# Order of the query blocks in the forgetting-attention branch: 0 to 7 against 0, 7, 1, 6, 2, 5, 3, 4

## The reference, cut to what matters

```python
c = jnp.cumsum(log_f, axis=1).transpose(0, 2, 1)
def block(i):                                   # i = 0..7, 128 queries each
    logits = einsum('bqhd,bkhd->bhqk', qb, k) * scale
    logits = logits + (cb[..., :, None] - c[..., None, :])
    logits = where(kpos[None, :] <= qpos[:, None], logits, -inf)
    p = softmax(logits, axis=-1)
    return einsum('bhqk,bkhd->bqhd', p, v)
```

## Time and profile before

| what | us |
|---|---|
| median of 3 runs | 1442.84 |
| the 3 runs | 1442.63, 1442.84, 1447.26 |
| the profiled execution | 1447.09 |
| its span, first to last instruction | 1445.2 |
| PE busy in the span | 1410.0 (98%) |
| DVE busy, ACT busy | 718.6 (50%), 689.4 (48%) |
| branch A, its first logits to its last pv | 660.5 to 893.3 |

### The profile page before, as it was taken

One profiled execution on the slowest core, in us unless ns is written; L12 is line 12 of the kernel. 1 busy time (PEld: TensorE's weight loads), 2 busy tenths in 40 slices (PEclk: granted clock), 3 DMA queues, 4 the chain that ended last, 5 costly groups with the idle time before them and its releaser, 6 DMA issues.

```text
span 1445.2 us, 21066 instructions
## 1 busy us (share of the span) xinstructions
PE 1410.0 (98%) x7910; PEld 1120.0 (77%) x7910; DVE 718.6 (50%) x1628; ACT 689.4 (48%) x1518; POOL 69.0 (5%) x136
## 2 busy tenths in 40 slices
PE   7999999999999999999999999999999999999998
PEld 7977677777767888887778777777777778888786
DVE  7558655555556785464433434633333355222633
ACT  7457866666763351114655565554454523113312
POOL 3132000000000000000000000000000000000100
PEclk9999999999999999999999999999999999999999
DMA  6155111111111222222010121112232131232522
GB/s 212 30 139 155 35 37 38 30 30 38 37 37 30 52 59 74 65 73 74 23 30 23 30 81 52 45 37 74 73 93 83 52 103 44 69 85 66 175 81 102
DMA packets 108019, 96.26 MB, mean 67 GB/s; under 512 B 8464, under 2 KB 93840, under 8 KB 107664
## 3 DMA queue, kind: packets, MB, share of 16 engines
q1 hardware_dynamic: 96672, 58.22, 14.9%
q0 software_dynamic: 11248, 36.71, 8.3%
HBM read 72.62 MB, written 18.09 MB: 63 GB/s over the span
## 4 chain that ended last, share of the span: by engine, by line
PE 84%; ACT 2%; DVE 2%; issue 1%; DMA 0%; DVEq 0%; ACTq 0%; POOL 0%; POOLq 0%
PE bank L855 20%; PE bank L857 20%; PE bank L856 20%; PE bank L1031 7%; PE bank L1050 6%; PE slot L1021 4%; PE slot L1006 2%; PE slot L855 1%; PE slot L856 1%; PE slot L857 1%; PE bank L975 1%; PE bank L1089 0%; DVE hs L1488 0%; ACT hs L1403 0%; PE bank L983 0%
## 5 line engine op out<-in xcount | busy, mean ns | idle before, releaser
L855 PE MATMUL bank<-hs,w_hl 128*128 128x512 f32 x1088 | 436.5, 401 | 0.4 <-issue 0.3
L857 PE MATMUL bank<-hs,w_hl 128*128 128x512 f32 x1088 | 426.6, 392 | 0.0
L856 PE MATMUL bank<-hs,w_hl 128*128 128x512 f32 x1088 | 425.5, 391 | 0.0
L1442 DVE TENSOR_TENSOR w_hl<-w_raw,w_hl 128x512 fp32r<-128x512 f32 (+1 forms) x168 | 113.8, 678 | 285.4 <-ACT w_hl L1141 284.4
L857 PEld LDWEIGHTS bank<-hs,w_hl 128*128 128x128 f32 x1088 | 205.0, 188 | 44.6
L855 PEld LDWEIGHTS bank<-hs,w_hl 128*128 128x128 f32 x1088 | 205.6, 189 | 41.3 <-issue 1.5
L856 PEld LDWEIGHTS bank<-hs,w_hl 128*128 128x128 f32 x1088 | 205.8, 189 | 39.8
L1141 ACT ACTIVATE w_hl<-w_raw 128x512 fp32r<-128x512 f32 (+1 forms) x168 | 103.9, 620 | 160.0 <-PE bank L857 152.1
L1469 DVE TENSOR_SCALAR_CACHE_REDUCE idle_out<-score,state 128x768 uint8<-128x768 f32 (+3 forms) x140 | 115.3, 824 | 4.8
L1649 DVE CUSTOM_DVE_ANT_0 slot<-slot,score 128x128 f32<-128x128 f32 (+7 forms) x64 | 47.4, 780 | 71.1 <-PE slot L1021 71.0
L1340 ACT ACTIVATE idle_out<-score,state 128x896 bf16<-128x896 f32 x64 | 70.3, 1098 | 11.6 <-DVE state L1465 10.3
(11 more groups left out here) (312 smaller groups left out, 2200.0 us busy)
## 6 DMA issues: line engine op xcount, KB each, us to landing
w_raw<-in_w_in_dram SPq DMA_DIRECT2D x136, 256.0 KB, 2.8
merged_scratch<-ms POOLq DMA_DIRECT2D x16, 512.0 KB, 3.5
ms<-merged_scratch POOLq DMA_DIRECT2D x16, 512.0 KB, 4.0
xn<-in_x_dram SPq DMA_DIRECT2D x8, 512.0 KB, 6.1
iq_st<-iq_hl POOLq DMA_DIRECT2D x32, 128.0 KB, 3.0
qb<-qb_scratch POOLq DMA_DIRECT2D x8, 512.0 KB, 5.2
w_raw<-in_w_o_dram SPq DMA_DIRECT2D x16, 256.0 KB, 3.8
qb_scratch<-bq_high POOLq DMA_DIRECT2D x4, 512.0 KB, 3.0
```

What stands on the lines that cost most here:

```text
L855: pe.matmul(out_, wh, mh, start=start, stop=False)
L856: pe.matmul(out_, wh, ml, start=False, stop=False)
L857: return pe.matmul(out_, wl, mh, start=False, stop=stop)
L1442: v.tensor_tensor(lo, src, hi.bitcast(F32), ALU.subtract).then_inc(w_low, 1)
```

## The change

The units of each head pair of branch A are listed in the order of query blocks 0, 7, 1, 6, 2, 5, 3, 4. Three places follow it: the filler of the last pair goes by the position in the pair and not by the block's number; the broadcasts for the first pair stand at steps 0, 0, 1, 1, because block 7 in step 1 reads all keys' gates; and DVE waits for the second half of the broadcasts at block 7. Branches B and C keep their order.

```diff
             elif x["br"] == "a" and x["ch"] == NCH["a"] - 1:
-                pump(1 if x["b"] >= 3 else 0)
+                pump(1 if s % TB >= 3 else 0)
...
-                    before.setdefault(at - 5 + i if ch else (0, 0, 2, 3)[i], []).append(bcast)
-            for b in range(TB):
+                    before.setdefault(at - 5 + i if ch else (0, 0, 1, 1)[i], []).append(bcast)
+            order = (0, 7, 1, 6, 2, 5, 3, 4) if br == "a" else range(TB)
+            for b in order:
...
-                        if a["br"] == "a" and a["b"] in (0, 4):
+                        if a["br"] == "a" and a["b"] in (0, 7):
```

## The result

The changed kernel is slower, by about 0.5%. Its median is 1451.57 us over 6 runs (1449.11 to 1456.11), that of before in the same comparison 1443.70 over 6 runs; the ratio is 1.0051, 95% interval 1.0036 to 1.0065. Two further sets gave 1449.45 (ratio 1.0036, 1.0022 to 1.0050) and 1451.17 (1.0041, 1.0026 to 1.0055). Over all 16 runs the median is 1450.76, that of 23 runs of before 1444.1.

What follows compares the result with a forecast made beforehand. PE, busy 98% of the span, was taken as the bound. New waits of +3.9 us in the last pair and 0.5 in the first, added to the median 1442.84, gave 1447.2 us, range 1442.0 to 1451.0.

Steps and rivals of the forecast that it cites:

- Last pair, item 1: Last pair's start: logits of block 7 wait 0.55 us for block 0's exps, starting 2.45 us after block 0's logits.
- Item 2: Last pair: turn of block 7 needs both its exps, at 8.55 us; PE waits 2.7 us, partly before block 0's pv.
- Item 3: Last pair: logits of block 6 need block 1's exps, queued behind ACT's copies; start at 12.95 us, a 1.9 us wait.
- Sum for the last pair: Last pair's waits 5.5 us, less 1.8 of before that go, plus 0.2 counted on both sides: +3.9 us.
- First pair, 0.5 us: First head pair: two broadcasts behind the value transposes share two banks; two PE waits, together 0.5 us, bounds 0 and 1.1.
- Head pairs 0 to 2, "no new wait": In pairs 0 to 2 filler in every step covers the latencies of blocks 7 and 6, so no new wait.
- The sum, +4.4 us: Branch A: last pair +3.9 and first pair 0.5; waits of steps 24 to 27 bounded by 4.0 and 6.3 us.
- The median of before as the base: The +4.4 us was added to the runs' median 1442.84, not to the profiled execution's 1447.09.
- The clock falls too: Rival: last pair's thinly used PE drops to half clock for about 7 us, giving 1449.6 us; chance 0.25 (1448 to 1451).
- My 2.4 for one fall: Price in us of one clock fall in the last pair: at most 3.4 lost, 2.4 taken since some time is waits anyway.
- the even mix: Rival: narrow units beside each wide one keep ACT and DVE from lagging, waits vanish, up to 2.6 us faster; chance 0.13.
- The waits were not half as long: Rival on the last pair: its chain starts earlier, waits only half as long, +1 to +2.5 us (1443.8 to 1445.3); chance 0.19.

Runs made afterwards that it cites:

- the last pair's order alone: New order only in branch A's last head pair, other pairs ascending as before: 1450.33 us, ratio 1.0035; with 13 unread matmuls added inside its two long waits, 1445.72 us, 1.0013.
- the fill: Unread extra matmuls inside PE's waits; here 13 in the last head pair's two long waits, added to the changed kernel: 1451.73 and 1449.20 us, ratio 1.0039 each.
- the pair of kernels with all waits filled: Changed kernel plus 13 unread matmuls in the last pair and 10 between branches C and A: 1448.84 us; kernel before plus those 10 only: 1444.14 us.

## Why the prediction was wrong, point by point

- *Last pair, item 1.* Right. Logits of block 7 were put 2.45 us behind those of block 0; they start at 846.32-843.90 = 2.42.
- *Item 2.* Right. The turn of block 7 was put at 8.55 and stands at 852.44-843.90 = 8.54. The waits before it are 0.47 and 1.94 us; the list gives 0.3 less than the 2.7 I gave, since the tails of the matmuls hide that much.
- *Item 3.* Right. The logits of block 6 were put at 12.95 and stand at 12.86.
- *Sum for the last pair.* A little high: +3.9 forecast, +3.23 in the trace; with the last pair's order alone it is +2.95, because then four group copies and the rest of the turn of 7 stand before the logits of 7 and cover block 0's exps.
- *First pair, 0.5 us.* Right, a little low: value transposes to logits take 663.42-661.15 = 2.27 us; before, the transposes took 0.97 to the next row and two broadcasts 0.64, so 0.66 are waits.
- *Head pairs 0 to 2, "no new wait".* Wrong by 0.2 us a pair, 0.6 to 0.7 in all: the turn of block 7 waits for the bank of the short pv ahead. I had looked for waits on slots and exps there, not on the ring.
- *The sum, +4.4 us.* Branch A is +4.62, with two errors that cancel: the last pair 0.7 too high, the other pairs 0.9 too low. That the sum is right to 0.2 is in part luck. Its bounds were also drawn a little wide: waits of 4.0 to 6.3 in place of 5.5 give 1445.7 to 1448.0, not 1445.5 to 1448.5. The two lowest runs with the fill, 1447.28 and 1447.40, are 4.7 us above the lowest level of before, 1442.6 to 1442.7.
- ***The median of before as the base.*** Here 1.3 us went missing (0.9 against the 1443.70 of the first comparison). The first three runs gave 1442.84; 23 runs give 1444.1. The level near 1442.6 is that of runs without any fall of the clock, and I took it for the middle. One of the three runs (1447.26) and the profiled execution (1447.09, two falls) said that there was more.
- ***The clock fall, left out of the sum.*** Together with the base this is the step that failed: "The clock falls too" had a chance of 0.25 and stood beside the forecast, not in it. It occurs in part of the runs and not in all or none, so it belongs to the sum as a mean. Against the same kernel's run without falls (1447.3) the 16 runs lie 3.7 us higher in the mean, those of before (23 runs, mean 1444.65, level 1442.6) 2.0 higher. The difference, 1.7 us, is my estimate of the mean price of the falls that the change adds; single ones in the last pair cost 1.5 and 3.8 us in the traces. My 2.4 for one fall was between. The Trainium skill (TensorE: Matmul & The Clock Gate, HAM oscillation), cited at this rival, has its example with idle gaps longer than the waits of 1.94 and 1.65 us here. The clock fell all the same in two traces, so the size and the chance had to come from runs.

4.6 of the waits and 1.7 of added falls make 6.3 us. That is no test of the split, since the 1.7 was taken from the same means (1450.98-1444.65 = 6.3; drawing the runs again at random gives 5.2 to 7.5, so the 1.7 is uncertain by about 1.2). The test is the pair of kernels with all waits filled, 4.7 us apart where those without the fill are 6.7 apart by the medians (1450.76-1444.1).

The forecast's range ended at 1451.0 because its base was 1.3 low and the falls only widened it. Chance had a part in the miss: the first six runs have their median at 1451.57, all 16 at 1450.76, just within the range.

Of the other rivals, the even mix did not win: PE's idle time in branch A rose from 2.00 to 5.80 us, and in the pairs with filler everywhere the new order still costs 1.30. The waits were not half as long either: 0.47 and 1.94 us where 2.7 in two pieces was forecast, and 1.65 where 1.9 was.

What is shown: that the waits are where and as long as worked out; that the clock falls in this stretch in two of the four traces without the fill that have the new order and the change's filler in the last pair, and in none of the four with it; and that more work inside the waits, with the same chain through ACT, brings back the runs without a fall. Counted at the lowest level of each order (1445.5 and 1447.3) there are none among 23 runs with the waits left idle (16 and 7), 9 among 24 with the 13 matmuls (7 of 12 with the last pair alone, 2 of 12 with the whole change), and 19 among the 65 of before (under 1443). This speaks for PE's idleness as the cause of the added falls. What stays open: how often it falls there in the whole changed kernel. The two sets with the 13 matmuls differ too little from the 16 runs without (2 of 12 against none of 16) to say it, and falls at two other places blur the count. The Trainium skill (TensorE: Matmul & The Clock Gate, What's actually happening) says that the activity watch is not tied to the kernel's start. The traces fit that, but can't show why: in one and the same stretch, its waits equal to 0.05 us, the clock fell in one trace of the changed kernel and not in two others.

## What to carry to other kernels

When units are reordered, the filler that covers their latency must be reordered with them. Here a good part of what the ascending order was worth was that narrow blocks stood where there was no filler.

Where PE is the bound, a new wait has two prices, its length and the chance that the clock falls behind it; the second is paid in part of the runs, and one trace or three runs can miss it. Take the base of a forecast from the runs' levels, not from the median of three.

Keeping PE busy inside its waits with matmuls that nobody reads is a clean test for the second price, since it leaves the chain as it is. It needs many runs where the clock falls at other places too; count the runs at the lowest level beside the median.

## What the runs showed of the hardware that was not expected

- 13 useless matmuls of 128x512 inside the last pair's waits lowered the median by 4.6 us (1450.33 to 1445.72), in part because those 12 runs had fewer falls elsewhere, and brought 7 of 12 runs to the lowest level, where none of 7 was. In the whole changed kernel the same fill moved the mean by only 0.8 us.
- The clock fell behind a stretch in which no single wait of PE was longer than 1.92 us (1.54 us of work in 3.50), and stayed low for 10.3 us once, though PE was busy for 8.70 of them; in the other trace it was low for less than 4 us.
- Run times of one kernel form levels: 1442.4 to 1442.9, about 1444.1 and 1446.9 or more for the kernel before. The uppermost vanished when the waits between branches C and A were filled; 3 of 12 runs then stood at 1445.7 to 1445.8.
